# Block inverses of a chunked delta rule: one trip through DRAM and a turn on TensorE in place of two trips

## What is computed

```
decay  = exp(where(tril, g_i - g_j, -inf))
lmat   = where(strict, einsum('nbhid,nbhjd->nbhij', k_beta, kc) * decay, 0)
tmat   = triangular_solve(eye + lmat, eye, lower, unit_diagonal)
u, w   = tmat @ v_beta,  tmat @ (k_beta * exp(g))
```

## Time and profile before

| | us |
|---|---|
| median of 3 runs (1925.04 to 1929.45) | 1925.65 |
| the profiled execution: time | 1924.74 |
| its span from first to last instruction | 1922.9 |
| PE busy | 1907.8 |
| PE's waits: for ACT's `kv`, 2 times | 5.9 |
| PE's waits: for POOL's `wl`, once | 1.8 |
| PE's waits: for POOL's `hl`, once | 0.5 |

### The profile page before, as it was taken

How to read it: one execution, slowest core, us unless ns; L and a number is a source line. 1 busy time by engine, 2 the same in 40 slices (tenths; PEclk the granted TensorE clock), 3 DMA queues, 4 the chain that set the end, 5 groups by cost and what they waited for, 6 DMA issues and landing times.

```text
span 1922.9 us, 25156 instructions
## 1 busy us (share of the span) xinstructions
PE 1907.8 (99%) x9674; PEld 1544.5 (80%) x9674; DVE 1195.3 (62%) x2078; ACT 905.1 (47%) x1415; POOL 708.9 (37%) x534
## 2 busy tenths in 40 slices
PE   9999999999999999999999999999999999999999
PEld 6878878777788878778777788777766788989989
DVE  6666756655745667666564747675544447867677
ACT  6453343343345454343344345587555445444453
POOL 5545432433355454432434455546222354000000
PEclk9999999999999999999999999999999999999999
DMA  5434442423535234532414545422211333323231
GB/s 203 129 114 150 130 134 82 155 75 113 195 106 174 99 115 148 164 105 67 165 66 137 186 148 151 160 84 88 69 55 56 117 103 121 113 74 123 86 110 66
DMA packets 94790, 227.70 MB, mean 118 GB/s; under 512 B 29936, under 2 KB 34032, under 8 KB 93360
## 3 DMA queue, kind: packets, MB, share of 16 engines
q1 hardware_dynamic: 88752, 222.95, 35.5%
q10 hardware_dynamic: 5920, 3.15, 0.6%
HBM read 193.95 MB, written 24.64 MB: 114 GB/s over the span
## 4 chain that ended last, share of the span: by engine, by line
PE 89%; DVE 6%; DMA 2%; ACT 1%; SPq 1%; issue 1%; POOL 0%; ACTq 0%; DVEq 0%
PE bank L466 88%; DVE kv L400 2%; DVE ER L400 2%; PE bank L470 1%; SPq L395 1%; DMA qk<-tmp 1%; DVE scs L425 1%; DMA kv<-blocks 1%; DMA inverses<-kv 0%; DVE m8s L422 0%; DVE tmp L410 0%; DMA st<-units 0%; DVE pads L410 0%; ACT wh L455 0%; DVE hl L400 0%
## 5 line engine op out<-in xcount | busy, mean ns | idle before, releaser
L400 POOL TENSOR_TENSOR wl<-st,wh 128x512 fp32r<-128x512 f32 x490 | 660.6, 1371 | 847.6 <-ACT wh L455 847.6
L466 PE MATMUL bank<-hh,wh 128*128 128x512 f32 x1616 | 649.1, 402 | 3.1 <-POOL wl L400 1.8
L466 PE MATMUL bank<-hh,wl 128*128 128x512 f32 x1616 | 629.1, 390 | 0.0
L466 PE MATMUL bank<-hl,wh 128*128 128x512 f32 x1616 | 628.9, 390 | 0.0
L455 ACT ACTIVATE wh<-st 128x1024 fp32r<-128x1024 f32 (+1 forms) x302 | 316.7, 1049 | 176.4 <-PE bank L466 126.1
L466 PEld LDWEIGHTS bank<-hh,wh 128*128 128x128 f32 x1616 | 303.3, 188 | 91.7 <-issue 24.9
L466 PEld LDWEIGHTS bank<-hl,wh 128*128 128x128 f32 x1616 | 303.6, 188 | 65.1 <-issue 5.0
L466 PEld LDWEIGHTS bank<-hh,wl 128*128 128x128 f32 x1616 | 303.3, 188 | 64.8
L400 DVE TENSOR_TENSOR xt<-xt,bank 128x512 f32<-128x512 f32 x80 | 54.9, 686 | 117.2 <-PE bank L466 117.2
L466 PE MATMUL bank<-fh,wh 128*128 128x256 f32 x448 | 126.8, 283 | 0.0
L466 PE MATMUL bank<-fl,wh 128*128 128x256 f32 x448 | 126.8, 283 | 0.0
(11 more groups left out here) (371 smaller groups left out, 2958.6 us busy)
## 6 DMA issues: line engine op xcount, KB each, us to landing
st<-units SPq DMA_DIRECT2D x300, 512.0 KB, 3.5
gates<-tmp SPq DMA_DIRECT2D x48, 256.0 KB, 3.6
gt<-gates SPq DMA_DIRECT2D x48, 256.0 KB, 3.6
pads<-tmp SPq DMA_DIRECT2D x32, 128.0 KB, 2.8
qk<-tmp SPq DMA_DIRECT2D x16, 256.0 KB, 4.3
x_scratch<-xt SPq DMA_DIRECT2D x2, 2048.0 KB, 8.5
xt<-x_scratch SPq DMA_DIRECT2D x2, 2048.0 KB, 8.3
ph<-phi SPq DMA_DIRECT2D x8, 512.0 KB, 4.7
```

What stands on the lines that cost most here:

```text
L400: return NOTHING if self.e is None else self.e.tensor_tensor(out, a, b, op)
L466: return NOTHING if self.e is None else self.e.matmul(out, lhsT, rhs, start=start, stop=stop, skip_group_check=share)
```

## The change

The substitution keeps `X` with the column first (`c i` in place of `i c`), so its result lies as `XT0` needs it, with the same number of operations on as many elements. The trip for `X0`, ACT's turned copy and ACT's six DMAs go. SP alone writes the result (step 30, behind the exchange of row 5, in runs of 512 floats) and reads `XT0` back (step 31, behind main step 39). In PE's step 34 sixteen turns of 128x128 make `X0` from `XT0` in banks 4 to 7, and ACT copies the four banks. PE waits for `XT0` in step 34, and for ACT's copies in step 35. POOL sets `XT0` alone to zero. In the first norm the last low half is made by DVE.

```diff
@@ vector: norm
-                if k > 0 and (k - 1) % 4 != 3:
+                if k > 0 and ((k - 1) % 4 != 3 or (w == "in" and k == 8)):
                     low_half(hl[:, k - 1, :], tmp[(k - 1) % 4][:], hh[:, k - 1, :], g, k - 1)
@@ pool: norm
-            low_part(7)
+            if w != "in":
+                low_part(7)
@@ tensor: delta
-            yield from idle(INVERSE)
+            yield from idle(INVERSE - 1)
+            pe.wait_ge(*at("xt0", l, 3))
+            for h in range(4):
+                o = bank(4 + h, "x0", l, h)
+                for i in range(4):
+                    t = pe.tr(o[:, sq4(i)], L.XT0r[:, h, i, :], identr[:])
+                t.then_inc(*sig("h_xt", l, h))
+            yield
...
-                pe.wait_ge(*at("x0", l, 3))
+                pe.wait_ge(*at(f"free{4 + h}", "x0", l, h))
@@ scalar: delta
-            yield from idle(INVERSE - BACK + 6)
-            ac.wait_ge(*at("inv", l, 31))
-            ac.cp(L.XT, L.X.rearrange("p i c -> p c i")).then_inc(*sig("h_xt", l))
...
-            yield from idle(BACK - 9)
+            yield from idle(INVERSE - 1)
+            for h in range(4):
+                ac.wait_ge(*at("h_xt", l, h))
+                ac.cp(L.X0[:, h, :, :].rearrange("p a b -> p (a b)"), banks[4 + h][:]).then_inc(*sig(f"free{4 + h}", "x0", l, h))
+            yield
@@ vector: delta
-                p = prod[:, 0:n * w].rearrange("p (i c) -> p i c", c=w)
+                p = prod[:, 0:n * w].rearrange("p (c i) -> p c i", i=n)
...
-                dv.tt(L.X[:, j + 1:32, 0:w], L.X[:, j + 1:32, 0:w], p, ALU.subtract).then_inc(*sig("inv", l, j + 1))
+                dv.tt(L.X[:, 0:w, j + 1:32], L.X[:, 0:w, j + 1:32], p, ALU.subtract).then_inc(*sig("inv", l, j + 1))
@@ sync: delta
-            yield from idle(INVERSE - BACK + 2)
+            yield from idle(INVERSE - BACK + 5)
             sp.wait_ge(*at("inv", l, 31))
             for f in range(2):
-                sp.dma(inv_d[:, :, :, 16 * f:16 * f + 16].rearrange("n q i c -> (n q) i c"), L.X[64 * f:64 * f + 64]).then_inc(*dma("inverses", l, f))
-            yield from idle(2)
-            sp.wait_ge(*at("x_zero", l, False))
-            sp.wait_ge(*at("inverses", l, 1))
+                sp.dma(invt_d[:, :, f, :].rearrange("n q c -> (n q) c"), L.inv[64 * f:64 * f + 64, 0, :]).then_inc(*dma("inverses_t", l, f))
+            yield
+            sp.wait_ge(*at("x_zero", l))
+            sp.wait_ge(*at("inverses_t", l, 1))
             for q in range(4):
                 r = slice(32 * q, 32 * q + 32)
-                sp.dma(L.X0[r, :, :, r].rearrange("p h b c -> p (h b) c"),
-                       inv_d[:, q, :, :].rearrange("n i c -> i n c")).then_inc(*dma("x0", l, q))
+                sp.dma(L.XT0[r, :, :, r].rearrange("p h b i -> p (h b) i"),
+                       invt_d[:, q, :, :].rearrange("n f (c i) -> (f c) n i", i=32)).then_inc(*dma("xt0", l, q))
             yield
         def gates(l, i):
```

More of the change, by code:

```diff
@@ L309 @@
 SHARED = {
-    "pe_heads": "dn_mm tp gl h_g h_kk dn_up on_up qk_up h_w h_kv h_r h_uw sc_w sc_s sc_o on_mm",
+    "pe_heads": "dn_mm tp gl h_xt h_g h_kk dn_up on_up qk_up h_w h_kv h_r h_uw sc_w sc_s sc_o on_mm",
     "pe_rows": "norm_mm qk_mm q2_mm k2_mm pl_mm lru_mm",
@@ L315 @@
     "act_small": "small_a lam_a f_sqa",
-    "act_heads": "dn_hi on_hi dn_sq dn_r on_sq on_r egl gexp h_eg h_dt h_vb h_xt",
+    "act_heads": "dn_hi on_hi dn_sq dn_r on_sq on_r egl gexp h_eg h_dt h_vb",
     "act_rows": "pl_p qk_sq qk_r qk_hi q2_sq q2_r k2_sq k2_r conv_0 conv2_0 conv_th zc_a pl_a ga_a gelu_a rec_a",
@@ L670, in build @@
     blk_d = nc.dram_tensor("blocks", [16, 4, 32, 32], F32).ap()
-    inv_d = nc.dram_tensor("inverses", [16, 4, 32, 32], F32).ap()
     invt_d = nc.dram_tensor("inverses_t", [16, 4, 2, 512], F32).ap()
@@ L706, in build @@
         L.M, L.inv = kv[:, 0:2, :].rearrange("p a (j i) -> p (a j) i", i=32), kv[:, 2:4, :]
-        L.X, L.XT = L.inv[:, 0, :].rearrange("p (i c) -> p i c", c=16), L.inv[:, 1, :].rearrange("p (c i) -> p c i", i=32)
+        L.X = L.inv[:, 0, :].rearrange("p (c i) -> p c i", i=32)
         L.aa4 = L.E + L.R
@@ L724, in build @@
         L.kfr, L.vfr = [sb(f"{n}fr{l}", [128, 4, T], F32R, stack=dr) for n in "kv"]
-        sb(f"dr_heads{l}", [128, 24 + 13 * 1024 + 8 + 640], stack=dr)
+        sb(f"dr_heads{l}", [128, 24 + 3 * 4 * T], stack=dr)
+        L.XT0r = sb(f"XT0r{l}", [128, 4, 4, 128], F32R, stack=dr)
+        sb(f"dr_behind{l}", [128, 5 * 1024 + 8 + 640], stack=dr)
         L.sq = [nacc, nr] + [sb(f"rsq{i}{l}", [128, T], stack=dr) for i in range(2)]
@@ L887, in low @@
     def low(g, k):
-        return at("hl_pool", g, k) if g[0] == "n" and k % 4 == 3 else at("hl", g, k)
+        return at("hl_pool", g, k) if g[0] == "n" and k % 4 == 3 and (g, k) != (feeds["in"], 7) else at("hl", g, k)
     def merged(l, n, m):
@@ L1110, in head @@
                     pe.wait_ge(*(at(f"free{s}", "R", l, h, n - 1) if n else at(f"free{s}", "W", l, h)))
-                    if n == 0:
-                        pe.wait_ge(*at("xt0", l, 3))
                     w = (128, 64, 32)[n]
@@ L2419, in delta @@
             dv.wait_ge(*at("inv", l, "zero"))
-            dv.set(eye[0:64, 0:256:17], 1.0)
-            dv.set(eye[64:128, 256:512:17], 1.0).then_inc(*sig("inv", l, 0))
+            dv.set(eye[0:64, 0:512:33], 1.0)
+            dv.set(eye[64:128, 16:512:33], 1.0).then_inc(*sig("inv", l, 0))
             yield from idle(INVERSE - BACK - 1 - len(CUTS))
@@ L2431, in delta @@
                 n, w = 31 - j, min(j + 1, 16)
-                p = prod[:, 0:n * w].rearrange("p (i c) -> p i c", c=w)
+                p = prod[:, 0:n * w].rearrange("p (c i) -> p c i", i=n)
                 dv.wait_ge(*at("inv", l, j))
-                dv.tt(p, L.M[:, j, j + 1:32].unsqueeze(2).broadcast_to([128, n, w]), L.X[:, j, 0:w].unsqueeze(1).broadcast_to([128, n, w]), ALU.mult).then_inc(*sig("inv", l, "p", j))
+                dv.tt(p, L.M[:, j, j + 1:32].unsqueeze(1).broadcast_to([128, w, n]), L.X[:, 0:w, j].unsqueeze(2).broadcast_to([128, w, n]), ALU.mult).then_inc(*sig("inv", l, "p", j))
                 dv.wait_ge(*at("inv", l, "p", j))
-                dv.tt(L.X[:, j + 1:32, 0:w], L.X[:, j + 1:32, 0:w], p, ALU.subtract).then_inc(*sig("inv", l, j + 1))
+                dv.tt(L.X[:, 0:w, j + 1:32], L.X[:, 0:w, j + 1:32], p, ALU.subtract).then_inc(*sig("inv", l, j + 1))
                 if j in CUTS:
@@ L3088, in delta @@
             L = layer[l]
-            for a in (L.X0, L.XT0):
-                gp.wait_ge(*at("quad", "gq", l, 0))
-                gp.set(a[:], 0.0).then_inc(*sig("x_zero", l, a is L.XT0))
+            gp.wait_ge(*at("quad", "gq", l, 0))
+            gp.set(L.XT0[:], 0.0).then_inc(*sig("x_zero", l))
             yield from idle(8)
```

## The result

The changed kernel takes 1930.49 us (median of 13 runs, 1929.18 to 1932.08), the kernel before 1925.53 (13 runs, 1924.31 to 1929.45). The ratio is 1.0023, with an interval of 1.0015 to 1.0030: 5 us slower, less than the 0.3% that were set as the bound of "no change". The forecast was 1929.4.

The account below looks back on a forecast made before the run. PE is 99% busy, so its few waits and the work it is given decide, not any engine's busy time. Gone 10.0 us, added 14.7: 1924.74 + 4.7 = 1929.4 us, range 1920 to 1936.

Parts of the forecast that it names:

- What goes: PE's waits of 3.17 and 2.75 us for ACT's copies, 1.82 for a weight's low half, 1.70 at half clock: 9.44 gone.
- First norm: Last low half made by DVE in 0.69 us where POOL needed 1.29: 0.6 us won.
- Turns: Added on PE: 32 turns of 128x128 at 0.086 us each, 2.76 us.
- Rival E: The turns on PE don't overlap: 8.0 us in place of 2.76, total 1934.7 us; chance 0.03.
- Waits: Added in step 34: PE waits for XT0 to land, 3.8 us in the first layer, 5.6 in the second.
- Rival D: XT0's four reads land 6.8 us behind their first issue, not 4.6: 2.2 more per layer, 1933.8 us; chance 0.13.
- Clock: Half clock behind PE's waits for XT0: 1.7 us behind the longer, 0.85 behind the shorter, 2.55 added.
- The sum: Gone 10.0 us, added 14.7, so 4.7 us slower than 1924.74: 1929.4 us.
- A: PE stands at the turn for 3 to 6 us in each layer; 1925.6 to 1933, middle 1929.4 us; chance 0.50.
- B: POOL's stretch holds neither substitution nor row 4's operations; PE waits 1.0 and 2.85 us, 1921.3 us; chance 0.22.
- C: XT0 lands before PE turns it, so only the turns are added; 1917.5 us; chance 0.12.

Follow-up runs that it names:

- turns_later: Changed kernel with everything behind the inverse (PE's turns and heads, ACT's copies, DVE's part of the heads) one step of delta later; 1917.58 us, ratio 0.9954.
- scalar_waits: Changed kernel with ACT's old wait for the substitution's end put back into step 30, without the copy and DMAs behind it; 1931.15 us, ratio 1.0026.
- write_ahead: Changed kernel with SP writing the inverses in step 27 and reading them in step 29, ahead of row 5's exchange and row 4's write; 1929.54 us, ratio 1.0017.
- sync_order_only: Kernel before with only SP's write of X three steps later, behind row 5's exchange, and X0 read back the step after; 1922.92 us, ratio 0.9980.

## Why the prediction came out right

**What goes**: right. None of the three waits is left.

**First norm**: right, 0.6 predicted and 0.64 measured; the wait for POOL's `hl`, 0.47, has gone. PE passes the place only 0.1 us earlier (36.47, not 36.59), since this execution lost 0.5 ahead of the norm, behind a wait for ACT's `hh` that the lists of most other runs don't have.

**Turns**: 2.76 predicted; at full clock 16 take 1.32 (237.43 to 238.75 in turns_later), 2.64 for both layers. Rival E is out.

**Waits**: 3.8 and 5.6 predicted, 4.47 and 4.14 measured, 8.6 in place of 9.4. The steps, first layer: the substitution ends at 228.57 (228.8), by the two operations foretold; the reads go out 4.55 behind it (3.5, range to 4.9), since POOL's second split held two of row 4's operations, 1.83 and 1.66, for 2.0 us together; they landed by 237.2, 4.1 behind the first issue (4.6). Rival D's 6.8 didn't occur, but its slower landing is possible: in scalar_waits and write_ahead the same reads took 4.2 and 3.6 from issue to landing. In the second layer two errors made up for one another in part. PE came at 802.86, not 800.1: I had worked its arrival out of the trace of before, without the delay of the first layer (2.7 us). And `XT0` landed at 807.1, 1.4 later than foretold, as the substitution ended at 798.77, 1.2 later: four of its operations were slow there, not two. An earlier split of POOL (from 788.45) caught the pair of 128x144 too, which took 1.40 and 1.28 us from 789.07 on, where before they took 0.30 and 0.31 from 789.98 on. So the wait came out at 4.14.

**Clock**: the term that was mis-sized. 1.7 + 0.85 = 2.55 were taken from the one row of 3.4 us at half clock. There were two stretches of 6.8, of which PE worked some 6.0 each: sixteen turns took 2.07 in place of 1.32, and the products from 239.35 to 243.20 lost half of 3.85: 0.75 + 1.9 = some 2.7 for each layer, 5.4 together. The single row of before was no scale for it, as the waits of 2.75 and 3.03 for the same copy show.

**The sum as measured**: -9.4 - 0.6 + 2.6 + 8.6 + 5.4 = 6.6 us, 0.5 lost ahead of the first norm, and 1.0 for DVE's `gt`: 8.1 against 7.3 between the spans; 0.8 stays open. The `gt` wait was 0.2 to 1.9 in single executions of other kernels, and isn't in the list of the kernel before, so I don't lay it to the change.

A, the forecast, held in its mechanism; B and C failed where the trace shows two long operations of DVE and PE standing at the turn. The sum itself missed by 2.6 us, 4.7 against 7.3 between the spans, the clock for 2.9 of them. That the time came within 1.1 us of the median is luck: the execution of after lies 1.6 above its own median, and that of before 0.8 below.

## What to carry to other kernels

A DMA round trip taken out of one engine's way moves the wait to the first instruction that needs its result: work out the landing against the consumer's arrival, and place the consumer behind it; one step later was worth 13 us here by the ratios, while three ways to have the data earlier were worth 4, 1 and -1, of which only the first is clear of the noise. A wait of PE is to be priced with the clock behind it, and that price is a range, taken from several executions. Freeing an engine (ACT) starts the work behind it (POOL's split), which may hold the very chain that is to become shorter.

## What the runs showed of the hardware

Around waits of PE of 2.7 to 4.6 us the granted clock stood at 0.50 for 6.8 us at ten places and for 3.4 at four, in part while PE still waited; behind the 2.75 of before it stayed at 1.00, as it did in the profiled execution with 48 turns in the wait. Two writes of 128 KB in runs of 16 floats (`inverses`, with ACT's writes of as much beside them) took SP 1.60 to 1.63 us to issue in both layers of the kernel before and in the first of sync_order_only, and 3.76 in the second; those in runs of 512 floats (`inverses_t`), alone, 1.10 to 1.12. What of it the runs are and what the company was not tried apart. Four reads of 64 KB landed 2.4, 3.6 or 4.2 us behind their issue (medians of the changed kernel, write_ahead and scalar_waits), with different transfers beside them.
